# One core of Trainium2: the order of chunks, splits and adaLN sums around the ends of the first layer of a two-block kernel

## What is computed

```
for l in range(2):
    shift, scale, gate = split(silu(c) @ ada_w[l] + ada_b[l], 3)      # adaLN, also for c_ctx
    h = rmsnorm(x, norm_g[l]) * (1 + scale) + shift                    # hc: the same for the context rows
    q, k, v, up, uf, g = split(h @ w_in[l])                            # context rows: all of it in layer 0
    mixed = concat([attention(q, k, v, kc, vc), pool(up), fourier(uf)])
    out = (mixed * silu(g)) @ w_out[l]
    x = x + gate * out                                                 # layer 0: the context rows too
```

## Time and profile before

| | us |
|---|---|
| median of 3 runs | 2336.55 |
| lowest, highest | 2335.84, 2337.86 |
| the profiled execution | 2333.01 |
| its span | 2331.2 |
| mean granted TensorE clock | 0.988 |

### The profile page before, as it was taken

How to read it: one execution, slowest core, us unless ns; L and a number is a source line. 1 busy time by engine, 2 the same in 40 slices (tenths; PEclk the granted TensorE clock), 3 DMA queues, 4 the chain that set the end, 5 groups by cost and what they waited for, 6 DMA issues and landing times.

```text
span 2331.2 us, 30004 instructions
## 1 busy us (share of the span) xinstructions
PE 2247.7 (96%) x11739; PEld 1835.9 (79%) x11739; DVE 1415.2 (61%) x2216; ACT 1038.6 (45%) x1590; POOL 271.2 (12%) x326
## 2 busy tenths in 40 slices
PE   5899999999999999999999998999999999999998
PEld 2477777788788767678888887888888888888887
DVE  3354533377688364546777776677755777567764
ACT  2232333332322254445554565555544555345553
POOL 1001100000011122100021324111100111001111
PEclk8999999999999999999999999999999999999999
DMA  9974433356655475635565544666656665666653
GB/s 356 331 262 171 149 122 120 114 184 196 211 176 176 165 266 191 218 102 169 189 217 178 180 137 157 189 190 188 186 196 190 187 189 182 197 188 183 190 190 117
DMA packets 322428, 437.14 MB, mean 188 GB/s; under 512 B 13848, under 2 KB 220112, under 8 KB 321264
## 3 DMA queue, kind: packets, MB, share of 16 engines
q1 hardware_dynamic: 316800, 413.19, 54.6%
q0 software_dynamic: 3392, 16.90, 2.0%
q10 hardware_dynamic: 2096, 5.15, 0.6%
HBM read 428.89 MB, written 6.29 MB: 187 GB/s over the span
## 4 chain that ended last, share of the span: by engine, by line
PE 86%; DVE 5%; ACT 3%; DMA 2%; issue 2%; POOL 1%; SPq 0%; ACTq 0%; POOLq 0%; DVEq 0%
PE ps L1382 25%; PE ps L1383 12%; PE ps L1357 8%; PE ps L1359 8%; PE ps L1358 8%; PE ps L1377 5%; PE ps L1379 5%; PE ps L1378 5%; PE ps L1337 2%; DVE SPL L1839 2%; ACT SPL L1595 2%; PE ps L1438 1%; PE ps L1455 1%; DMA RAW<-in_w_in_dram 1%; DMA RAW<-in_ada_w_dram 1%
## 5 line engine op out<-in xcount | busy, mean ns | idle before, releaser
L1839 DVE TENSOR_TENSOR SPL<-RAW,SPL 128x1024 fp32r<-128x1024 f32 x592 | 749.0, 1268 | 537.2 <-ACT SPL L1595 534.8
L1382 PE MATMUL ps<-HS,SPL 128*128 128x512 f32 x2688 | 954.5, 399 | 11.0 <-DVE SPL L1839 8.1
L1595 ACT ACTIVATE SPL<-RAW 128x1024 fp32r<-128x1024 f32 x592 | 622.2, 1056 | 478.1 <-PE ps L1359 170.2
L1383 PE MATMUL ps<-HS,SPL 128*128 128x256 f32 x2688 | 754.0, 280 | 0.0
L1382 PEld LDWEIGHTS ps<-HS,SPL 128*128 128x128 f32 x2688 | 506.2, 188 | 134.9 <-DVE SPL L1839 5.7
L1383 PEld LDWEIGHTS ps<-HS,SPL 128*128 128x128 f32 x2688 | 509.1, 189 | 2.0 <-issue 1.7
L1357 PE MATMUL ps<-SPL,HS 128*128 128x512 f32 x960 | 396.8, 413 | 13.4 <-DVE SPL L1839 5.3
L1359 PE MATMUL ps<-SPL,HS 128*128 128x512 f32 x960 | 377.4, 393 | 0.0
L1358 PE MATMUL ps<-SPL,HS 128*128 128x512 f32 x960 | 376.9, 393 | 0.0
L1357 PEld LDWEIGHTS ps<-SPL,HS 128*128 128x128 f32 x960 | 182.2, 190 | 76.1 <-issue 17.3
L1358 PEld LDWEIGHTS ps<-SPL,HS 128*128 128x128 f32 x960 | 182.6, 190 | 41.5 <-issue 6.0
(11 more groups left out here) (291 smaller groups left out, 1834.6 us busy)
## 6 DMA issues: line engine op xcount, KB each, us to landing
RAW<-in_w_in_dram SPq DMA_DIRECT2D x208, 512.0 KB, 4.9
RAW<-in_ada_w_dram SPq DMA_DIRECT2D x192, 512.0 KB, 4.9
RAW<-in_ffn_w_up_dram SPq DMA_DIRECT2D x192, 512.0 KB, 3.6
RAW<-in_w_out_dram SPq DMA_DIRECT2D x96, 512.0 KB, 4.6
RAW<-in_ffn_w_down_dram SPq DMA_DIRECT2D x96, 512.0 KB, 4.2
x_spill<-XT POOLq DMA_DIRECT2D x2, 2048.0 KB, 14.3
XT<-x_spill POOLq DMA_DIRECT2D x1, 4096.0 KB, 13.0
MM<-in_x_dram ACTq DMA_DIRECT2D x2, 1024.0 KB, 11.4
```

The costliest lines, as they stand in the source:

```text
L1382: mm(PS[b][:, :], wr, hh, start=k == 0, stop=False, skip_group_check=True)
L1383: m = mm(PS[b][:, 256:512], wl, hh[:, 0:256], start=False, stop=k == KT - 1, skip_group_check=True)
L1595: act(SPL[:, (n - 1) % NSPL, 0, :], raw_of(i), ACT.Copy).then_inc(s_hi, 1)
L1839: tt(w[:, 1, :], raw_of(s["i"]), w[:, 0, :].bitcast(F32), ALU.subtract).then_inc(s_lo, 1)
```

## The change

Four edits. First, the 16 m2 tiles are split four at a time, behind the first three chunks of the last gate group and at the border, and no longer all at the border. Second, the 24 chunks of sums_a stand beside main chunks 38 to 61 instead of 40 to 63, and those of sums_b beside out's chunks 0 to 23 instead of 4 to 27; sums_b may write into MM once 8 of the 16 tiles are split. Third, the adaLN chunks on PE are dealt out anew, with the same 80 in all: 38 instead of 40 in layer 0's in, 2 behind its last gate chunk, 2 behind each of out's chunks 24 to 27 instead of 4 behind the last, 8 instead of 4 at the border to layer 1 (FILL), and 24 instead of 32 in layer 1. Fourth, by these numbers two groups end elsewhere: one on PE at the border between in and out, one at the border between out and front.

```diff
--- before.py
+++ after.py
@@ -19,7 +19,7 @@
 NSPL = 4
 AHEAD = 5
 START_AHEAD = 3
-FILL = 4
+FILL = 8
 GATES = (8, 10, 0, 2, 4, 6, 12, 14), (8, 10, 12, 14, 0, 2, 4, 6)
 BW = [112, 120, 64, 96, 96, 96, 96]
 OFFS = [sum(BW[:b]) for b in range(7)]
@@ -889,15 +889,21 @@
                 x["maps"] = [list(x["ended"]), list(x["ended"])]
                 hi.extend([idle, idle, ends, idle, sums, load_tables, idle, idle, rstd, idle, tables] + [context_row] * 5)
 
+            def split_mixed(q):
+                for k in range(4 * q, 4 * q + 4):
+                    put("m2", k=k, last=[gated[k], multiplied()])
+
             def project(upto):
+                if both:
+                    for q, main in enumerate(ends0[:3]):
+                        run_chunks(main)
+                        split_mixed(q)
                 run_chunks(upto)
                 flush(hi)
                 flush(low)
-                last = multiplied()
                 if both:
-                    put("back", last=[last, (s_accT, 3), (s_gm, KT), (s_gs, KT)])
-                    for k in range(KT):
-                        put("m2", k=k, last=[gated[k], last])
+                    put("back", last=[multiplied(), (s_accT, 3), (s_gm, KT), (s_gs, KT)])
+                    split_mixed(3)
                 need["out", l] = (lambda k: [(s_m2, k + 1)]) if both else (lambda k: [gated[k]])
 
             if both:
@@ -1114,19 +1120,22 @@
         left = [c for g in range(8, 12) for c in ada_group(0, g)] + [c for g in (0, 7) for c in ada_group(1, g)]
         gates1 = [c for g in range(8, 12) for c in ada_group(1, g)]
         sums_a = [c for g in (4, 1, 5) for c in ada_sums(1, g, 2, 1, lambda: [(s_fm, 4)])]
-        sums_b = [c for g in (2, 6, 3) for c in ada_sums(1, g, 2, 0, lambda: [(s_m2, KT)])]
+        sums_b = [c for g in (2, 6, 3) for c in ada_sums(1, g, 2, 0, lambda: [(s_m2, 8)])]
         marks = []
 
         def lay_out(cs):
             chunks.extend(cs)
             marks.append(len(chunks))
 
-        lay_out(main0[0] + mixed(main0[1][:40], left) + [c for pair in zip(main0[1][40:], sums_a) for c in pair])
-        lay_out(outs0[:4] + [c for pair in zip(outs0[4:], sums_b) for c in pair] + left[:4] + outs0[28:])
-        del left[:4]
+        behind = lambda main, sums: [c for pair in zip(main, sums) for c in pair]
+        lay_out(main0[0] + mixed(main0[1][:38], left) + behind(main0[1][38:62], sums_a) + main0[1][62:] + left[:2])
+        del left[:2]
+        ends0 = [chunks.index(c) + 1 for c in main0[1][60:]]
+        lay_out(behind(outs0[:24], sums_b) + [c for i in range(4) for c in [outs0[24 + i]] + left[2 * i:2 * i + 2]] + outs0[28:])
+        left = gates1
         lay_out(left[:FILL])
         del left[:FILL]
-        lay_out(mixed(main1[1], gates1))
+        lay_out(mixed(main1[1], left))
         lay_out(outs1)
         lay_out([c for g in range(2) for c in group("tm", "in2", W2, 1024 + g * 512, alt(g), v_out2(g, alt(g)), TILES[:2], side=2)])
         lay_out([c for i in range(4) for c in group("fm", "in2", W2, i * 256, alt(i), u_out(2 * i, alt(i)), side=2)])
```

## The result

| | us |
|---|---|
| the changed kernel, median of 6 runs | 2348.73 (2345.32 to 2353.11) |
| the kernel before, 6 runs beside them | 2335.18 (2331.12 to 2337.86) |
| ratio | 1.0062, 95% interval 1.0049 to 1.0075 |
| the changed kernel's profiled execution | 2347.18 |
| forecast | 2344.2, range 2337 to 2350 |

The change makes the kernel 0.6% slower, 13.6 us between the medians and 14.2 between the two profiled executions. The direction and the places were as forecast, the amount was not: 7.7 us were.

What follows compares the result with a forecast made beforehand. PE, busy 96% of the span, was taken as the bound, so only its idle and half clock could move. B +3.6, sums sooner 0, C +2.2, D +3.1, E -1.2 make +7.7 on 2336.55: 2344.2 us, range 2337 to 2350.

Steps and rivals of the forecast that it cites:

- B: Border of layer 0's in to out: m2 wait goes, sum_turn waits on DVE; +3.6 us, bounds +1.5 and +5.2.
- T: Moment in the profile before when sum_turn starts behind the last gate chunk, 611.16 us.
- C: Border of out to front: a PE group's turn waits for L1910 on DVE; +2.2 us, bounds +0.5 and +3.
- D: Border to layer 1: w_in's loads wait for buffers held by adaLN chunks; +3.1 us, bounds +1 and +4.7.
- T2: Moment in the profile before when the FILL chunks start at the border to layer 1, 805.99 us.
- third rival: Loads decide: D +4.7 with the clock, B +5.2, C +3, E 0; +12.9 us, 2349.5; chance 0.12.
- E: Inside layer 1: the 2.33 us column wait goes, 1.1 returns through the attention chain; -1.2 us, bounds -2.6 and 0.
- second rival: A wash: idle grows as computed but the clock holds at B and C; +0.4 us, 2337; chance 0.18.
- The first (faster): Waits at the borders and in layer 1 give way, no clock falls; -7.0 us, 2329.5; chance 0.08.

Runs made afterwards that it cites:

- e1: The changed kernel with the last two chunks of the adaLN group on PE ending between in and out moved 24 main chunks earlier; 2341.67 us, ratio 1.0036.
- e5: e1 with the 8 chunks on PE in out put four behind chunk 24 and four behind chunk 25, none at the border to front; 2336.63 us.
- e7: The changed kernel run once more without edits, for a second profile; 2348.12 us (2 runs).
- e8: The kernel before run once more without edits, for a second profile; 2335.13 us (8 runs).
- e9: The changed kernel with in as in e1, out's 4 adaLN chunks behind its chunk 24, FILL = 4, 32 chunks in layer 1; 2332.25 us, ratio 0.9977.
- e10: The kernel before with tiles split four by four and the 4 PE chunks ahead of front moved behind out's chunk 24; 2330.15 us, ratio 0.9975.
- e6: The kernel before with tiles split four by four, sums_b beside out's chunks 0 to 23, front's 4 PE chunks behind out's chunk 24; 2339.13 us, ratio 1.0016.

## Why the prediction was right in direction and short by half

The time lay in the range, and the mechanism of three of its four places was the one forecast. Some of that is luck: the kernel before ran 1.4 us faster beside the changed one (2335.18) than the 2336.55 that the forecast adds to, and the measured 13.6 us on 2336.55 would be 2350.1, at the upper edge.

B: the turn of the PE group, the queue behind the four products and the 3 us idle came as worked out (L1432 at T + 6.40 for T + 6.6). Wrong was the size of its clock terms: I took half of 1.84 us for a slow sum_turn and 0.4 more for out. sum_turn ran slow in full (3.57 for 1.84, 1.7 us for my 0.9), and 12 matmuls of out behind it too (1.0 us more than before for my 0.4); 5.1 us of clock, 0.7 of it during the idle, where before has 1.7. The upper bound I had given, +5.2, was the better value. I also named the four products wrongly (sums_a for sums_b). It did not change the time, since L1882 stands behind them either way, but it left the reader with a false cause, which e1 cleared.

C: right in cause and amount, +2.0 for +2.2, the wait 3.8 us with front's first chunk at half clock. I had counted 1.7 us for that clock and 0.3 more than before; 3.4 us were lost, but half of it during the idle. e5 shows that the turn alone is the cause.

D: right, by its own terms. What the forecast rests on is when rows h(3) are there, T2 + 14.8 for PE; it was T2 + 14.96, and the difference grew by 5.4 us for 5.3. The clock fell at half during the chunk between, and that only filled the wait, as the third rival's counter-argument said: +3.3 to +3.7 for +3.1. The first load's time (issued at T2 + 1.09, used 3.80 later, 3.78 before) was right to 0.02.
The fit of the Trainium skill, "DMA: Bandwidth & Descriptors", section "Anatomy of one DMA", an estimate of 3.2 us for 512 KB on another issuing path, is 0.6 short of both.

E: the step that failed. I let 1.2 us be won where the column's wait of 2.33 goes, and took back 1.1 for the attention chain. The column's wait went, and the 1.6 us at 854 with it; the chain took back all of it, so that PE idles 10.3 us there, where it idled 10.4. With 1.7 us of clock lost in a stage that before ran at full clock it became +1.2, and in e7, with 5.1, +4.1.

The second block: no term. 2.6 us were lost there in a part of the program that the change doesn't touch, by a half clock at 1457; e7 has it as well, e8 half of it. e8, which is the kernel before, lost 3.0 us there against its own first profile, so these 2.6 us cannot be put down to the change. The prediction counted the clock at the new idles only and took the old ones for fixed. What it should have said: every old idle of 1.4 to 2.3 us in the program is a lot, with some 1.7 us or more to win or lose.
The Trainium skill, "TensorE: Matmul & The Clock Gate", section "Part 1: The HAM clock gate", has this rule, that the watch runs free of the program; e8 agrees, with 0.62 behind an idle of 1.86 us that had 1.00 in the first profile. The prediction cited it and did not let it into the old idles.

The second rival (the clock holds at B and C) was refuted in both profiles. The first (faster) has been built in e9 and e10: where sum_turn has no wait the border does gain 4.3 us, as that rival counted.

## What to carry to other kernels

A group of work whose end needs a turn on PE, a copy on ACT and a reduction on DVE should not end where PE runs out of other work: its latency is then bare, and each idle of some 3 us costs a portion or more of half clock (1.7 us each, less what falls into the idle) on top. Fill for such a border is not free either when it takes every buffer of the ring from which the next stage is loaded. Before a move is costed, read for every wait what is queued on its engine ahead of the instruction that releases it, and what a bookkeeping count takes in (e6).

## What the runs showed of the hardware

The loss by half clock comes in equal portions of 1.7 us of full-speed time. It came with or behind every idle of 2.6 us or more (50 of them in twelve profiles from 100 us on, the longest 6.53 us), and behind idles of 1.36, 1.86 and 2.23 us in one execution and not in another of the same program. Half clock during an idle or a wait costs nothing: at front 3.4 us were lost and 1.7 of them shown. The same kernel's executions differ by up to 12 us (2332.0 to 2344.35 for before on one chip); a change of 3 us is seen in a trace at its place and hardly in a median. A lone adaLN chunk on PE costs 0.84 us beside a pair (1.91 less 1.07), a chunk of a pair 0.53 (1.07 / 2).
